# A decoder trunk on one core: layer 0 reads x channel by token and applies the norm factors behind its projections

## The reference, cut to what matters

```
h = rmsnorm(x, norm_in[0])              # per token: x * rsqrt(mean(x*x) + eps) * gain
c_q, c_kv, k_pe, z = split(h @ w_in)    # 256, 256, 64 and 1024 columns
c_q, c_kv = rmsnorm(c_q), rmsnorm(c_kv) # per token again
k_pe = rope(k_pe);  gate = silu(z)
```

## Time and profile before

| what | value |
|---|---|
| median of three runs | 1403.82 us (1402.02 to 1404.79) |
| the profiled execution, its own time | 1403.35 us |
| its span in the trace | 1401.6 us |
| PE busy / PE weight loads / DVE / ACT / POOL | 94% / 80% / 58% / 40% / 38% |
| granted TensorE clock, mean | 0.983 |
| DMA moved | 110.59 MB, 79 GB/s on average |

### The profile page before, as it was taken

How to read it: one execution, slowest core, us unless ns; L and a number is a source line. 1 busy time by engine, 2 the same in 40 slices (tenths; PEclk the granted TensorE clock), 3 DMA queues, 4 the chain that set the end, 5 groups by cost and what they waited for, 6 DMA issues and landing times.

```text
span 1401.6 us, 19020 instructions
## 1 busy us (share of the span) xinstructions
PE 1320.1 (94%) x6976; PEld 1126.5 (80%) x6976; DVE 812.5 (58%) x1512; ACT 553.8 (40%) x1116; POOL 527.5 (38%) x720
## 2 busy tenths in 40 slices
PE   5999989999999899999996999899989998999997
PEld 4888878889898788888875788778878997888886
DVE  4442455455555515425577889997977776345333
ACT  4322234444444303213334555566166666023122
POOL 3732014544444635324601023224055664744301
PEclk9999999999999899999999999999999999999999
DMA  7222241211110332224400122233123211422112
GB/s 218 61 75 83 90 131 55 71 46 54 46 53 23 134 104 68 72 61 128 136 8 0 31 90 76 91 114 119 46 83 91 76 61 60 129 94 72 57 64 83
DMA packets 82220, 110.59 MB, mean 79 GB/s; under 512 B 9297, under 2 KB 45393, under 8 KB 82129
## 3 DMA queue, kind: packets, MB, share of 16 engines
q1 hardware_dynamic: 82128, 109.38, 25.0%
HBM read 81.56 MB, written 27.79 MB: 78 GB/s over the span
## 4 chain that ended last, share of the span: by engine, by line
PE 76%; DVE 12%; ACT 4%; issue 3%; POOL 3%; DMA 1%; DVEq 0%; POOLq 0%; SPq 0%; ACTq 0%
PE psum L1466 22%; PE psum L1468 22%; PE psum L1467 22%; PE psum L1622 4%; PE psum L1606 2%; PE psum L1483 2%; DVE xr L1331 2%; DVE gz L1355 2%; DVE p L1157 1%; ACT psum L1049 1%; DVE p L1153 1%; POOL p L984 1%; DVE p L1154 1%; ACT p L1115 1%; POOL small L983 1%
## 5 line engine op out<-in xcount | busy, mean ns | idle before, releaser
L1466 PE MATMUL psum<-ring_hi,act_lo 128*128 128x512 f32 x816 | 325.8, 399 | 9.9 <-issue 5.8
L1468 PE MATMUL psum<-ring_hi,act_hi 128*128 128x512 f32 x816 | 321.6, 394 | 0.0
L1467 PE MATMUL psum<-ring_lo,act_hi 128*128 128x512 f32 x816 | 321.5, 394 | 0.0
L974 POOL CAST ring_hi<-raw 128x512 fp32r<-128x512 f32 x128 | 84.9, 664 | 353.6 <-DMA raw<-in_dsa_w_in 153.4
L1145 DVE TENSOR_TENSOR act_lo<-psum,act_hi 128x512 fp32r<-128x512 f32 (+3 forms) x292 | 166.1, 598 | 70.8 <-ACT act_hi L1004 48.7
L1466 PEld LDWEIGHTS psum<-ring_hi,act_lo 128*128 128x128 f32 x816 | 155.9, 191 | 42.3 <-issue 6.0
L1004 ACT ACTIVATE act_hi<-psum 128x512 fp32r<-128x512 f32 (+3 forms) x260 | 123.7, 517 | 156.3 <-PE psum L1622 84.5
L977 POOL TENSOR_TENSOR ring_lo<-raw,ring_hi 128x512 fp32r<-128x512 f32 x128 | 180.3, 1409 | 10.3
L1468 PEld LDWEIGHTS psum<-ring_hi,act_hi 128*128 128x128 f32 x816 | 155.5, 191 | 33.2
L1467 PEld LDWEIGHTS psum<-ring_lo,act_hi 128*128 128x128 f32 x816 | 156.0, 191 | 31.5
L983 POOL TENSOR_TENSOR small<-small 128x1 f32<-128x1 f32 x128 | 70.5, 550 | 247.1 <-ACT p L1115 181.8
(11 more groups left out here) (226 smaller groups left out, 2499.4 us busy)
## 6 DMA issues: line engine op xcount, KB each, us to landing
raw<-in_dsa_w_in SPq DMA_DIRECT2D x48, 256.0 KB, 3.0
gz<-z_scratch SPq DMA_DIRECT2D x16, 512.0 KB, 3.5
raw<-in_ple_w_gate SPq DMA_DIRECT2D x32, 256.0 KB, 3.2
raw<-in_mla_w_in SPq DMA_DIRECT2D x24, 256.0 KB, 3.0
xr<-in_x SPq DMA_DIRECT2D x8, 512.0 KB, 6.1
z_scratch<-gz SPq DMA_DIRECT2D x16, 256.0 KB, 2.0
pe_scratch<-t SPq DMA_DIRECT2D x8, 512.0 KB, 3.5
raw<-in_mla_w_out SPq DMA_DIRECT2D x16, 256.0 KB, 3.3
```

Of the source, the lines that this page charges most:

```text
L974: last = nc.gpsimd.tensor_copy(dst, src[:, c0:c0 + cols])
L1466: nc.tensor.matmul(dst, lhs(1), rhs(0), start=start, stop=False)
L1467: nc.tensor.matmul(dst, lhs(0), rhs(1), start=False, stop=False)
L1468: return nc.tensor.matmul(dst, lhs(0), rhs(0), start=False, stop=stop)
```

## The change

Only the input side of layer 0 is changed.

- x comes a second time as `x_t`, channel by token, laid out outside the kernel; layer 0 loads it in 16 tiles of 128 channels x 512 tokens (256 KB each), first the eight of tokens 0 to 511 ("half 0"), then those of half 1. The gain comes as 8 columns (`gcol`) in place of a row on all partitions.
- `x_split`: ACT writes the hi part of x times gain straight from the loaded tile, DVE the lo part. There are no transposes, no `norm_a` and no `norm_b` in layer 0's input.
- `x_square`: squares of each tile (ACT for half 0, DVE for half 1), added up over the eight channel tiles by POOL, 7 additions of 128 x 512 for each half. `tok`: PE sums over partitions with 4 small matmuls against a column of ones (placed at the seventh channel tile of the group, or of job 4), DVE copies, POOL makes four factors at a time.
- Jobs c of tokens tiles 0 to 3 are one group: for each channel tile all four take it in turn, in the four banks of ring A. Jobs 4 to 7 follow one by one.
- The factors go in later: into the squares and factors of the c jobs (one more POOL instruction each), and for kpe and z by a DVE multiplication of the bank with `rs_row`, a row of factors on all partitions. `rb` makes that row behind job 5: ACT and DVE build 8 diagonal blocks, PE multiplies them with ones (4 matmuls), ACT copies the two banks.
- The kpe and z weight tiles stand elsewhere in the list; the last two of the z chunk stand behind `tables`.

The core of the diff (the order of the list first, then the engines' parts):

```diff
     first = chunk_of(0, 0)
-    norm0(0)
-    for d in range(3):
+    for d in range(KD):
+        x_split(0, d)
         w(first, d)
...
+        if d:
+            x_square(0, d - 1)
+    x_square(0, KD - 1)
+    for d in range(KD):
+        x_split(1, d)
+        x_square(1, d)
     add("small_loads", {"const_ld": 2, "lat_ld": 2})
...
+    group, sums = [], tok(0)
+    for t in range(4):
+        group.append(c_job(t, group=group, parts=x_parts[0], tok=sums))
+    for d in range(4):
+        w(next_chunk(0, 0), d)
+    sums = tok(1)
+    for t in range(4, T):
+        c_job(t, group=None, parts=x_parts[1] if t == 4 else None, tok=sums if t == 4 else None)
+        if t == 4:
+            for d in range(4, KD):
+                w(next_chunk(0, 0), d)
+        else:
+            for d in (2 * t - 10, 2 * t - 9):
+                w(next_chunk(0, 1), d)
+        if t == 5:
+            add("rb", {"dg_hi": 1, "dg_lo": 1, "b_full": 2, "rb": 2}, ring="B", jobs=2, freed=["rb"])
...
     tb = add("tables", {"stage": 2, "trig": 2, "cs_st": 1})
-    fk = [key_job(0, 1, job).after["fk"] for job in range(2)]
+    fk = []
+    for job in range(2):
+        fk.append(key_job(0, 1, job).after["fk"])
+        w(next_chunk(0, 1), 6 + job)
```

```diff
 # POOL
+                elif k == "x_square" and n["d"]:
+                    half, d = n["half"], n["d"]
+                    pool.wait_ge(sem["xsq%d" % half], s.after["xsq%d" % half])
+                    if s.before["xacc"]:
+                        pool.wait_ge(sem["xacc"], s.before["xacc"])
+                    nc.gpsimd.tensor_tensor(sq_acc(half), sq_acc(half), sq_slot(half, d), ALU.add).then_inc(sem["xacc"], 1)
+                elif k == "tok":
+                    c = 4 * n["half"]
+                    pool.wait_ge(sem["tok_ms"], s.after["tok_ms"])
+                    linked(nc.gpsimd.tensor_scalar(mean[:, c:c + 4], ms[:, c:c + 4], 1.0 / D, EPS, ALU.mult, ALU.add))
+                    for t in range(c, c + 4, 2):
+                        last = nc.gpsimd.tensor_tensor(rs[:, t:t + 2], mean[:, t:t + 2], minus_half, ALU.pow)
 # ACT
+                elif k == "rb":
+                    act_e.wait_ge(sem["tok_rs"], 2)
+                    for t in range(T):
+                        last = nc.scalar.activation(kpe[0][:, t * P:(t + 1) * P], ident[:], ACT.Copy,
+                                                    scale=rs[:, t:t + 1])
+                    last.then_inc(sem["dg_hi"], 1)
...
                     elif name == "c":
+                        t = n["job"]
                         act_e.wait_ge(sem["a_full"], s.after["a_full"])
+                        act_e.wait_ge(sem["tok_rs"], 1 + t // 4)
 # DVE
+                if k == "x_split":
+                    d, half = n["d"], n["half"]
+                    dve.wait_ge(sem["hi"], s.after["hi"])
+                    nc.vector.scalar_tensor_tensor(act_at(1, d, half * CW, CW), x_at(d, half), gcol[:, d:d + 1],
+                                                   act_at(0, d, half * CW, CW).bitcast(F32),
+                                                   ALU.mult, ALU.subtract).then_inc(sem["lo"], 1)
+                elif k == "x_square" and n["half"] == 1:
...
+                    nc.vector.tensor_tensor(sq_slot(1, d) if d else sq_acc(1), x_at(d, 1), x_at(d, 1),
+                                            ALU.mult).then_inc(sem["xsq1"], 1)
...
+                elif k == "rb":
+                    dve.wait_ge(sem["dg_hi"], 1)
+                    for t in range(T):
+                        at = slice(t * P, (t + 1) * P)
+                        last = nc.vector.scalar_tensor_tensor(kpe[1][:, at], ident[:], rs[:, t:t + 1],
+                                                              kpe[0][:, at].bitcast(F32), ALU.mult, ALU.subtract)
+                    last.then_inc(sem["dg_lo"], 1)
 # PE
+                if k == "rb":
+                    pe.wait_ge(sem["dg_lo"], 1)
```

More of the change, by code:

```diff
@@ L202, in proj, with x_split, x_square @@
         return s
[L205 to L208, removed]
+    add("start", {"gcol_ld": 1, "consts": 1})
+    def x_split(half, d):
+        s = add("x_split", {"x_ld%d" % (half * KD + d): 1, "hi": 1, "lo": 1}, half=half, d=d)
+        x_parts[half].append(s.after["lo"])
+        for t in range(4 * half, 4 * half + 4):
+            lo_at[("act", t)] = s.after["lo"]
+    def x_square(half, d):
+        add("x_square", {"xsq%d" % half: 1, "xacc": 1 if d else 0}, half=half, d=d)
+    x_parts = [[], []]
     def z_chunk(lay, i, base, prefetch=True, extra=None):
@@ L685, in build @@
         tri_r = sb("tri_r", P, F32R)
+        ones_r = sb("ones_r", P, F32R)
+        gcol = sb("gcol", KD)
         xr = sb("xr", T * D)
@@ L714, in build @@
         rs = small[:, 16:24]
-        lat_ms, lat_mean, lat_rs = small[:, 24:28], small[:, 28:32], small[:, 32:36]
+        lat_ms, lat_mean, lat_rs = small[:, 96:104], small[:, 104:112], small[:, 112:120]
+        one = small[:, 120:121]
         minus_half = small[:, 36:38]
@@ L1472, in bank_free, with token_sums @@
                     pe.wait_ge(sem[name], v)
+            def token_sums(s):
+                half = s.n["half"]
+                pe.wait_ge(sem["consts"], 1)
+                pe.wait_ge(sem["xacc"], s.n["acc"])
+                bank_free(s)
+                for i in range(4):
+                    last = nc.tensor.matmul(bank(s.banks[0])[:, i:i + 1], sq_acc(half)[:, i * P:(i + 1) * P], one,
+                                            start=True, stop=True)
+                last.then_inc(sem["b_full"], 1)
             for s in steps:
                 k, n = s.kind, s.n
-                if k == "norm_b":
+                if k == "rb":
+                    pe.wait_ge(sem["dg_lo"], 1)
+                    for j in range(2):
+                        bank_free(s, j)
+                        for part in (1, 0):
+                            last = nc.tensor.matmul(bank(s.banks[j]), ones_r[:], kpe[part][:, j * CW:(j + 1) * CW],
+                                                    start=part == 1, stop=part == 0)
+                        last.then_inc(sem["b_full"], 1)
+                elif k == "norm_b":
                     pe.wait_ge(sem["xn"], n["xn"])
@@ L1532, in _ @@
                     name, b, buf = n["name"], s.banks[0], n["buf"]
+                    if name == "c" and n["group"]:
+                        if n["job"]:
+                            continue
+                        for d in range(KD):
+                            pe.wait_ge(sem["lo"], n["parts"][d])
+                            pe.wait_ge(sem[n["w_ready"][d][0]], n["w_ready"][d][1])
+                            if d == KD - 2:
+                                token_sums(n["tok"])
+                            for one_of in n["group"]:
+                                if d == 0:
+                                    bank_free(one_of)
+                                t = one_of.n["job"]
+                                last = product(bank(one_of.banks[0]), lambda part: act_at(part, d, t * P, P),
+                                               lambda part: w_at(part, buf, d, 0, CW), d == 0, d == KD - 1)
+                                if d == KD - 1:
+                                    last.then_inc(sem["a_full"], 1)
+                        continue
                     bank_free(s)
-                    pe.wait_ge(sem["lo"], n["act"])
+                    if not n["parts"]:
+                        pe.wait_ge(sem["lo"], n["act"])
                     if n["half"] is not None:
```

150 lines of the change are left out of this document (100 added, 50 removed).

## The result

The changed kernel takes 1428.91 us (median of 4 runs, 1426.69 to 1429.79) where before takes 1402.92 on the same chip: ratio 1.0188, 95% interval 1.017 to 1.0206. That is 26.0 us slower; forecast were 19.7 more, 1423. The profiled execution spans 1427.4 us, 25.8 over before's 1401.6, so the spans can be compared piece by piece. The mean granted clock of the span is 0.969 against 0.983. Two executions in all were disturbed, one of before beside the first four experiments (1889.97 us) and the profiled one of the third experiment (7.4 ms); their times are left out.

A forecast was written before the change was run, and what follows sets the result against it. PE, busy 94% of the span, was taken as the bound. Later c jobs 9.3, the first z job's wait 8.9 and z jobs 1.5 sum to 19.7 us slower: 1403.4 to 1423 us, 8-in-10 range 1411 to 1430.

The forecast's parts named there:

- wait at `rb`: Behind c job 5, PE waits for the diagonal blocks of ACT and DVE: 7.2 us, between 5.1 and 8.5.
- E: End of the c jobs: 70.65 us before the change, forecast 79.9, which is 9.3 us later.
- What is gained: At the start PE begins at 6.4 us, 12.9 earlier; transposes between jobs go, 5.2 us; 18 us on PE.
- The clock: PE's matmuls at half clock behind waits: 2.2 us booked for the start and each new wait over 3 us.
- DVE against POOL: In the squares' additions the two engines take turns: 2.3 us for each channel tile, 2.7 at most.
- The wait behind the group: c job 4 waits for bank 0, with `tok(0)` behind all 14 POOL additions: 14.0 us, starting at 45.0.
- The first z job: Loads of z tiles 6 and 7 wait for the second sine: 6.7 us and 2.2 for half clock, 8.9.
- The z jobs: DVE's multiplication ahead of each SiLU is hidden except at two existing waits: 1.5 us lost.
- No turns: Rival: DVE and POOL don't delay each other at the additions; job 4 at 37.6, +8.2, 1411.5 us; chance 0.12.
- Heavy turns: Rival: each DVE or POOL instruction holds for its listed time; job 4 at 50, +27, 1430 us; chance 0.17.
- The sums in time: Rival: job 4 starts at 31 without waiting for the factors; not slower, -0.6, 1402.8 us; chance 0.08.
- The loads as a bound: Rival: 512 KB loads per channel tile limit the start; held hidden below 2.3 us a tile; no chance of its own.

The follow-up runs named there:

- first four experiments: Four variants of the changed kernel: z tiles 6 and 7 moved, `rb` cut, half 1's squares on ACT, factors before those squares; 1420.92, 1416.3, 1418.94, 1415.99 us.
- third experiment, experiment 3: Changed kernel with half 1's squares made by ACT instead of DVE; 1418.94 us, ratio 1.0127 to before.
- experiment 4: Changed kernel with `tok(0)` and jobs 0 to 3 ahead of half 1's squares, PE's part of `rb` behind the kpe jobs; 1415.99 us, ratio 1.0104.
- tenth kernel: Reordered kernel with half 1's squares on ACT and later table store, its first three z tiles moved behind job 5 from ahead of `tok(1)`; 1398.73 us, ratio 0.9992.
- Experiment 1: Changed kernel with z weight tiles 6 and 7 ahead of `tables` instead of behind; 1420.92 us, ratio 1.0137 to before.
- ninth kernel: Changed kernel without the DVE multiplication of the z banks by the factor row; 1425.11 us, ratio 1.0175 to before.
- the last three: Reordered kernels with half 1's squares on ACT: z tiles spread, then the first three behind job 5, then tiles 6 and 7 before tables; 1397.2, 1398.73, 1397.2 us.
- eleventh kernel: The tenth kernel with z weight tiles 6 and 7 ahead of the tables instead of behind; 1397.2 us, ratio 0.997 to before.
- the eighth: Reordered kernel with kpe and z weights split by ACT and DVE, plus half 1's squares on ACT, z tiles spread, tables stored later; 1397.2 us, ratio 0.9982.

## Why the prediction was right, and where its sizes were off

The sign, the mechanism and the three places were right. Off were sizes, by 25.8 - 19.7 = 6.1 us of span: 1428.91 lies at the upper edge of the forecast's own range (1416 to 1429). The working of the forecast and the trace of after, piece by piece (us; a half clock behind a wait counts to the piece behind it):

| piece | forecast | measured |
|---|---|---|
| start | 6.4 | 7.40 |
| group of four jobs | 24.6 | 25.16 |
| wait at job 4 | 14.0 | 15.48 |
| jobs 4 and 5 | 13.7 | 14.46 |
| wait at `rb` | 7.2 | 7.86 |
| `rb`, jobs 6 and 7 | 14.0 | 13.57 |
| E | 79.9 | 83.93 |
| E to `key_back` | 25.2 | 24.33 |
| loss from there to the end of the z jobs | 1.5 | 4.5 |

**What is gained.** ACT's start was mis-sized. Rows of ACT after, timeline:

```profile
3.85 1.28 ACT L1077 ACT_TABLE_LOAD   x1 [3.85 <-DMA xr<-in_x_t]
5.15 0.72 ACT L1077 ACTIVATE act_hi<-xr,gcol 128x512 fp32r<-128x512 f32 x1
```

The load was there at 3.85, sooner than the 4.3 that I took, but a table load of 1.28 us stands behind it, ahead of the first piece. +1.0. The trace of before has that load too, where it costs nothing:

```profile
0.72 1.28 ACT L1013 ACT_TABLE_LOAD   x1 [0.72 <-PEq L1646]
```

There it ran while ACT still had 2.46 us to wait for x; after the change it ran when the wait was over. ACT waits for two semaphores ahead of its first instruction now (`gcol_ld` and the tile's own), for one before; whether that is the reason is not shown.

**The clock** fell behind each of the three waits, as booked: 128x512 matmuls stand at half clock from 48.63, 70.95 and 105.3 for 2.6 to 6 us, and from 7.97 at the start. The 2.2 us booked for each were 2.4 at job 4, 1.6 at `rb` and about 3.2 in the first z job, half of that behind `key_back`. The whole trace has 93 such matmuls, that of before 59.

**The group** was fed, and slower by 0.6.

**DVE against POOL.** The turn was right (2.33 for 2.3); experiment 3 bears out its two parts. Wrong was to take 2.3 for every tile of half 0. DVE and ACT in half 0 of after:

```profile
12.66 1.78 DVE L1295 TENSOR_TENSOR ring_lo<-raw,ring_hi 128x512 fp32r<-128x512 f32 x1
14.37 1.78 DVE L1266 SCALAR_TENSOR_TENSOR act_lo<-xr,gcol,act_hi 128x512 fp32r<-128x512 f32 x1
17.08 0.63 ACT L1097 ACTIVATE ring_hi<-raw 128x512 fp32r<-128x512 f32 x1 [0.77 <-DMA raw<-in_mla_w_in]
21.18 0.63 ACT L1097 ACTIVATE ring_hi<-raw 128x512 fp32r<-128x512 f32 x1 [2.33 <-DMA raw<-in_mla_w_in]
23.50 0.94 DVE L1266 SCALAR_TENSOR_TENSOR act_lo<-xr,gcol,act_hi 128x512 fp32r<-128x512 f32 x1 [0.77 <-ACT act_hi L1077]
```

POOL's first addition came only at 10.84, and then it had one ready for each DVE instruction, so both of a tile took a turn of 1.7 us (12.66, 14.37): 3.4 a tile. DVE frees the slots of `raw`, so two weight loads came late, and ACT waited 0.77 and 2.33 for them. Half 1 started at 23.50, not 21.5. I had the loads as hidden below 2.3 us a tile; they are hidden only while DVE frees slots at that pace.

The Trainium skill, page "SBUF — State Buffer", section "SBUF: two separate sides", has the port pair locked for a whole instruction, the loser fully blocked. The alternation here is of that kind, but an estimate from it and the listed durations (1.29 and twice 0.69) would be 2.7 us for a tile, and the trace has 2.33: the measurement decides.

**The wait behind the group.** From half 1's start to the last addition 18.7 were forecast and 19.3 measured, from there to job 4 4.8 and 5.2. All of the 3.0 us by which job 4 is late (48.04 for 45.0) is thus half 0's 2.0 and these. That the cause is the order and not the number of turns, experiment 4 shows: with the same additions behind the factors, the wait is 2.86. The prediction named POOL's queue alone; experiment 4 moved the squares in DVE's queue too, which had held the copy of the sums to 41.38, and no run parts the two.

**The wait at `rb`** was 0.7 over its 7.2, inside its bounds. ACT and DVE after, timeline:

```profile
63.45 2.43 ACT L1088 ACTIVATE kpe_hi<-ident,small 128x128 fp32r<-128x128 f32 x8
65.92 4.39 DVE L1283 SCALAR_TENSOR_TENSOR kpe_lo<-ident,small,kpe_hi 128x128 fp32r<-128x128 f32 x8
```

ACT's eight small pieces cost 0.30 each, not 0.16 to 0.25, and DVE's 4.39 in all beside POOL's splits; in the tenth kernel, where POOL splits nothing, they take 2.19. So 2.2 us of this wait are turns.

**The first z job.** 24.33 against 25.2: right, with the sine at E + 14.9 (14.2 forecast). Experiment 1 shows what makes it: with the two loads ahead of the tables it is gone.

**The z jobs** were the largest miss for their size. The waits grew little, at 159.64 from 0.2 to 1.00 and at 219.01 from 1.69 to 2.05. But PE's clock then fell. PE after, timeline:

```profile
219.78 0.40 PE L1590 MATMUL psum<-ring_hi,head_w_lo 128*128 128x512 f32 x1
220.58 0.63 PE L1590 MATMUL psum<-ring_hi,head_w_lo 128*128 128x512 f32 x1
221.01 0.63 PE L1591 MATMUL psum<-ring_lo,head_w_hi 128*128 128x512 f32 x1
223.88 0.39 PE L1592 MATMUL psum<-ring_hi,head_w_hi 128*128 128x512 f32 x1
```

Some 8 matmuls stand 0.43 apart instead of 0.23, 1.6 us; before has none there. Another 1.4 is half clock that runs on past `key_back` to 111.31. With 0.8 and 0.4 of waits that is 4.2 of the 4.5. The ninth kernel shows what hangs on the multiplication: 3.1 us. I booked the clock only behind waits over 3 us.

**The rivals.** No turns fell with the 2.33 and 1.70. Heavy turns gave 1430, which lies nearer to the total than my 1423, but by spacings of 2.7 in half 1 that are not there. Half 0, where both DVE instructions of some tiles took a turn, was slower than I had it, and that is part of why the total came out near that rival. The sums in time fell at job 4. The loads as a bound, which had no chance, had a small share, through DVE.

What stays open is whether a version without any wait up to `key_back` can be had; the last three each moved one wait of 4 to 5 us to the next place. The copies of the factor row ahead of the tables would be the next thing to try.

## What to carry to other kernels

Moving work off the busiest engine gains only what the in-order queues behind it can follow: ask for each new small result (here two norm factors) what stands ahead of it in every queue that it passes, and put it ahead of bulk work that nobody waits for yet. A wait that is removed uncovers the next chain with a time of its own (tables, their store, the loads behind it), so add up the ends of all chains at a point, not the waits of one trace. Where DVE and POOL both work on SBUF alone, count one turn for each pair of instructions, and count who frees the load slots.

## What the runs showed of the hardware

- DVE instructions with two SBUF inputs and POOL's additions take turns, one of each: 1.70 us for a pair of 128x512, where alone they take 0.69 and 1.26. Small DVE pieces are held up as well: eight 128x128 pieces 4.39 us beside POOL's splits, 2.19 alone.
- ACT's first table load (1.28 us) may or may not be hidden behind the wait for the first data: in before it ran from 0.72, while ACT waited for x until 4.46; in after it began at 3.85, when the wait was over.
- Whether the clock falls behind a wait of about 2 us is not fixed: behind 2.05 us at 219.01 it fell in after, behind 2.20 at 190.76 it did not in the eleventh kernel, behind 2.24 at 190.03 it did not in the eighth, and behind 2.19 at 190.55 it did in the tenth.
